# Three edits to the order of work in a one-core diffusion step: output weight splits one query tile later, one tile evicted ahead of the next, a silu table loaded ahead of its use

## The reference

```python
for i in range(DEPTH):
    hp = rms_norm(xp, norm_pre[i, 0]) * (1.0 + sc1_p) + sh1_p
    hs = rms_norm(xs, norm_pre[i, 0]) * (1.0 + sc1_s) + sh1_s
    # i == 0: retention_mixer, i == 1: mla_context / mla_latent (attention), ending in "@ w_out"
    xp = xp + rms_norm(yp, norm_post[i, 0]) * g1_p
    xs = xs + rms_norm(ys, norm_post[i, 0]) * g1_s
    hp = rms_norm(xp, norm_pre[i, 1]) * (1.0 + sc2_p) + sh2_p
    hs = rms_norm(xs, norm_pre[i, 1]) * (1.0 + sc2_s) + sh2_s
    fp = expert_choice_ffn(hp, moe_w_router[i], moe_w_gate[i], moe_w_up[i], moe_w_down[i])
    fs = expert_choice_ffn(hs, moe_w_router[i], moe_w_gate[i], moe_w_up[i], moe_w_down[i])
    xp = xp + rms_norm(fp, norm_post[i, 1]) * g2_p
    xs = xs + rms_norm(fs, norm_post[i, 1]) * g2_s
# an expert: (silu(tokens @ w_gate) * (tokens @ w_up)) @ w_down
```

## Time and profile before

| | us |
|---|---|
| median of three runs | 2384.13 (2383.55 to 2388.96) |
| the profiled execution | 2390.39 |
| its span, first to last instruction | 2388.6 |

### The profile page before, as it was taken

How to read it: one execution, slowest core, us unless ns; L and a number is a source line. 1 busy time by engine, 2 the same in 40 slices (tenths; PEclk the granted TensorE clock), 3 DMA queues, 4 the chain that set the end, 5 groups by cost and what they waited for, 6 DMA issues and landing times.

```text
span 2388.6 us, 27244 instructions
## 1 busy us (share of the span) xinstructions
PE 2265.5 (95%) x10016; PEld 1552.2 (65%) x10016; DVE 1757.0 (74%) x1949; ACT 1273.6 (53%) x1348; POOL 194.9 (8%) x226
## 2 busy tenths in 40 slices
PE   6999999999988999999999798999989999999995
PEld 2866868768654666666666455777656666666663
DVE  2675675766766899999989634455478989999996
ACT  3321312212235777877777434444357777877773
POOL 1000000000022000111000110000120101110001
PEclk9999999999998999999999899999999999999998
DMA  7442434425435999999999400001169999999991
GB/s 270 124 141 92 155 123 133 151 87 176 132 130 197 341 356 362 352 359 345 350 336 362 147 36 3 6 31 37 75 232 352 350 346 361 368 343 345 339 353 60
DMA packets 167652, 529.15 MB, mean 222 GB/s; under 512 B 13525, under 2 KB 22282, under 8 KB 167306
## 3 DMA queue, kind: packets, MB, share of 16 engines
q1 hardware_dynamic: 162954, 515.35, 60.1%
q0 software_dynamic: 2304, 8.39, 1.0%
q10 hardware_dynamic: 2304, 4.20, 0.5%
HBM read 516.72 MB, written 11.17 MB: 221 GB/s over the span
## 4 chain that ended last, share of the span: by engine, by line
PE 89%; DVE 4%; ACT 3%; issue 1%; POOL 1%; DMA 0%; SPq 0%; POOLq 0%; ACTq 0%; DVEq 0%
PE ps L1738 85%; PE ps L1741 4%; POOL SMALL L608 0%; POOL SMALL L607 0%; ACT W_HI L338 0%; DVE IDX L1433 0%; DVE B L1259 0%; DVE X L1260 0%; ACT W L338 0%; DMA REGION<-in_ada_b_dram 0%; DVE MIXREG L1432 0%; DVE B L1234 0%; DVE ROUTE L1435 0%; ACT QN_HI L338 0%; ACT B L751 0%
## 5 line engine op out<-in xcount | busy, mean ns | idle before, releaser
L1470 DVE TENSOR_TENSOR W_LO<-RAW_W,W_HI 128x2048 fp32r<-128x2048 f32 x384 | 867.5, 2288 | 76.4 <-ACT W_HI L338 72.7
L338 ACT ACTIVATE W_HI<-RAW_W 128x2048 fp32r<-128x2048 f32 x384 | 726.9, 1918 | 192.5 <-PE ps L1738 191.5
L1738 PE MATMUL ps<-W_HI,XET_HI 128*80 128x512 f32 x1024 | 322.3, 396 | 7.4 <-DVE B L1504 5.8
L1738 PE MATMUL ps<-W_HI,XET_LO 128*80 128x512 f32 x1024 | 319.6, 393 | 0.0
L1738 PE MATMUL ps<-W_LO,XET_HI 128*80 128x512 f32 x1024 | 319.6, 393 | 0.0
L1738 PEld LDWEIGHTS ps<-W_HI,XET_HI 128*80 128x80 f32 x1024 | 150.9, 148 | 89.1 <-DVE B L1504 6.7
L1738 PEld LDWEIGHTS ps<-W_LO,XET_HI 128*80 128x80 f32 x1024 | 151.9, 148 | 85.8 <-issue 0.9
L1738 PEld LDWEIGHTS ps<-W_HI,XET_LO 128*80 128x80 f32 x1024 | 152.0, 148 | 84.6 <-issue 0.9
L1203 DVE SCALAR_TENSOR_TENSOR ADA_SUM<-ADA_RAW,NCOL,ADA_SUM 128x512 f32<-128x512 f32 x280 | 191.2, 747 | 0.3 <-DMA ADA_RAW<-in_ada_w_dram 0.3
L1738 PE MATMUL ps<-W_HI,HTE_HI 128*80 128x512 f32 x512 | 166.9, 407 | 8.6 <-issue 8.6
L1738 PE MATMUL ps<-W_LO,HTE_HI 128*80 128x512 f32 x512 | 161.2, 396 | 0.0
(11 more groups left out here) (270 smaller groups left out, 3494.3 us busy)
## 6 DMA issues: line engine op xcount, KB each, us to landing
RAW_W<-in_moe_w_gate_dram SPq DMA_DIRECT2D x128, 1024.0 KB, 5.7
RAW_W<-in_moe_w_up_dram SPq DMA_DIRECT2D x128, 1024.0 KB, 6.0
RAW_W<-in_moe_w_down_dram SPq DMA_DIRECT2D x128, 1024.0 KB, 5.2
ADA_RAW<-in_ada_w_dram SPq DMA_DIRECT2D x80, 512.0 KB, 3.6
RING_RAW<-in_ret_w_in_dram SPq DMA_DIRECT2D x48, 512.0 KB, 4.6
W<-in_ada_w_dram SPq DMA_DIRECT2D x4, 2048.0 KB, 13.9
RING_RAW<-in_ret_w_out_dram SPq DMA_DIRECT2D x16, 512.0 KB, 4.8
xn_rows<-B SPq DMA_DIRECT2D x8, 512.0 KB, 12.7
```

The lines of the kernel that those rows point to most:

```text
L338: return nc.scalar.activation(out, in_, ACT.Copy, scale=scale)
L1470: V_.tensor_tensor(W_LO[:, slot], RAW_W[:, slot], W_HI[:, (place + i) % HSLOTS].bitcast(F32), ALU.subtract).then_inc(MS_["lo"], 1)
L1738: return T.matmul(out, lhsT, rhs, start=first, stop=last)
```

## The change

VectorE's `split_out(h, t)` at the end of turn (h, t) becomes `split_out(h, t - 1)`, for t of 1 and more; the four splits after the last head stay, and ScalarE's WO_HI stay in their turns. In the joint, for tile 0 alone, ScalarE's four evictions go ahead of the squares of tile 1, and VectorE's four evictions go between the scaling and the addition of tile 1. In each mixture ScalarE takes the silu of one column of `SSU` (a column that nothing reads any more and that is written anew later) behind the token splits of the first pair, which moves the load of the silu's table to that place.

```diff
@@ -957,6 +957,8 @@
                 split_tokens(0, 0, None)
                 split_tokens(0, 1, None)
+                act.wait_ge(ru_ss, NT * 2 * layer + NT)
+                nc.scalar.activation(SSU[:, 0:1], SSU[:, 0:1], ACT.Silu)
@@ -1009,8 +1011,11 @@
                 for t in range(NT):
                     squares(t + 2)
                     if not layer:
+                        if not t:
+                            norm_act_tile(n + 1, 1, 0, t)
                         norm_squares(n + 1, t + 1, x_ready, NT * n + t + 2)
-                        norm_act_tile(n + 1, 1, 0, t)
+                        if t:
+                            norm_act_tile(n + 1, 1, 0, t)
                         if t >= 2:
                             latent_rows(t - 2)
@@ -1250,13 +1255,15 @@
-            def update(n, t, Y):
+            def update(n, t, Y, between=None):
 
                 if 0 <= t < NT:
                     dve.wait_ge(ru_rstd, NT * n + t + 1)
                     if t == 0:
                         dve.wait_ge(gate_ev, 4 * (n + 1))
                     chain.link(V_.scalar_tensor_tensor(Y[:, t, :], Y[:, t, :], RSTDU[:, t:t + 1], GATE[:, t // NLAT, :], ALU.mult, ALU.mult))
+                    if between:
+                        between()
                     V_.tensor_tensor(X[:, t, :], X[:, t, :], Y[:, t, :], ALU.add).then_inc(x_ready, 1)
@@ -1573,9 +1580,12 @@
                     if not layer:
                         normalise(n + 1, t)
-                    update(n, t + 1, YB2)
-                    if not layer:
-                        norm_dve_tile(n + 1, 1, 0, t)
+                    if not layer and not t:
+                        update(n, t + 1, YB2, lambda: norm_dve_tile(n + 1, 1, 0, 0))
+                    else:
+                        update(n, t + 1, YB2)
+                        if not layer:
+                            norm_dve_tile(n + 1, 1, 0, t)
@@ -1700,7 +1710,8 @@
                         if t == 0 and h:
                             head_out(h - 1, 0)
-                        split_out(h, t)
+                        if t:
+                            split_out(h, t - 1)
                         if h == MH - 1 and t == 0:
                             heads_lo(1, 0, 0, 4)
                 split_out(MH, 0)
```

## The result

The changed kernel takes 2375.84 us, the median of 7 runs (2374.48 to 2380.68). The kernel before, timed beside it, takes 2388.51, also 7 runs (2383.55 to 2389.95). The ratio is 0.9949, with a 95% interval of 0.9940 to 0.9959. The forecast was 2373.2, with a range of 2367.5 to 2378.5. As a ratio to its own starting point it was 2373.2 / 2384.13 = 0.9954. The profiled run of after took 2374.86 us, where that of before took 2390.39; the two are 15.5 us apart.

The account below looks back on a forecast made before the run. TensorE, carrying 89% of the chain that ended last, was taken as the bound. Head 5's 4.96 + head 7's 3.2 + joint's 2.5 + table's 0.2 = 10.9 us off the median 2384.13 gave 2373.2, range 2367.5 to 2378.5.

Parts of the forecast that it names:

- Head 5: Attention head 5: later weight splits remove VectorE's stall, so it lasts as head 6; 4.96 us, 1.63 of it clock.
- Head 7: Attention head 7: TensorE's waits before the transposes of tiles 2 to 4 go; 3.2 us, bounds 2.2 to 3.5.
- the new wait: Head 7: TensorE's products wait for WO_LO of tile 2's block, 0.4 us.
- Joint: First mixture to attention: tile 0's evictions go first, so its products start 2.5 us earlier; 2.5 us taken.
- Table: First expert of each mixture: earlier silu table load gains 0.1 us each, 0.2 in all.
- the move from the profiled execution to the median: Whole kernel: the 10.9 us from the profiled execution, 2390.39, taken equally off the median, 2384.13, giving 2373.2.
- The clock keeps its share: Rival: head 5's 1.63 us absent from the median's executions, joint keeps 1.2; 8.0 us, 2376.1; chance 0.15.
- the order on VectorE does nothing: Rival, heads 5 and 7: WO_HI is late anyway, only joint and table remain; 2.7 us, 2381.4; chance 0.05.
- WO_LO becomes the last thing in head 7: Rival: a new wait in head 7 eats its 3.2 us; gain 7.7, 2376.4; chance 0.08.
- slower case: Joint's products stay at 1.2 GHz past tile 0, through four further tiles; 2401.6 us; chance 0.03.
- the two cases that the sum weighed: Joint: clock returns as long after the restart as before, 2.5 us, or at the same moment, 1.2 us.
- early-clock rival: Joint: the clock returns early in tile 0's products; 13.9 us in all, 2370.2; chance 0.10.

Follow-up runs that it names:

- e1: Kernel before with only VectorE's weight splits one query tile later: 2381.47 us against 2389.45, ratio 0.9964.
- e9: Kernel before with products that nothing reads in three TensorE idles of the attention's preparation: 2386.05 us, ratio 0.9987.
- e8: Changed kernel with VectorE's multiplication ahead of the W_LO that the silu overlaps, first turn of each mixture: 2379.5 us, one run.
- e10: Kernel before with the joint's edit and unread products in the preparation's three idles: 2385.42 us, ratio 0.9986.
- e11: Changed kernel with the multiplication ahead of W_LO and unread products in the idles of preparation, mixtures, last combines and joint: 2366.29 us, ratio 0.9905.

## Why the prediction was right, point by point

- **Head 5**, 4.96 predicted, 4.97 between the two profiled runs. Comparing with the next head was the whole working. It gave the price in that one run: 3.2 us of wait, which every run has, and 1.63 us of clock, which five of nine do not have.
- **Head 7**, 3.2 predicted, 3.43 measured; the new wait was put at 0.4 and is 0.47. The walk by the ends of earlier steps was right to 0.3 us. Both terms together, 8.2, came out as 8.40 between the two profiled runs (heads 5 to 7 in the table) and as 8.0 in e1's time; against the other runs that keep the stall empty it is 6.7 to 9.1.
- **Joint**, 2.5 predicted. The start of the products, worked out from the ends of the evictions, was right (2.39 in after, 2.48 in the idle). Its worth was not one number: tile 1's transposes come 3.02 us earlier in after, the time within either group falls by about 2.3, and on top of e9 by 0.6. In the profiled runs with the whole edit the stretch to the gates is shorter than 70.3 by 2.9 (three runs), 2.2 (e8, 68.13) and 1.1 (e10). The price ahead, 1.35 us later for tile 1, stayed covered: its transposes have no idle.
- **Table**, 0.2 predicted, 2 x 0.13 in the trace.
- **The step that was wrong** was the move from the profiled execution to the median. The prediction found 6.26 us between them and no row that said where, and took off the same 10.9. The table shows two places, by the runs of the lower group that keep the stall (table alone, joint alone). The preparation takes 67.48 us in before and 64.99 there. The twelve products of head 5 take 5.14 in before and 3.51 there; head 7 takes 0.8 more instead, so heads 5 to 7 are worth 7.6 us there, not 8.4. If the runs of after are parted by eye at their gap (four to 2375.84, three from 2378.29), the change is worth about 2384.5 - 2375.0 = 9.5 us in the lower and 2389.8 - 2379.5 = 10.3 in the upper group. So 12.7 us between medians are some 10 of the change and the rest a different share of the groups. That the time came so close was in part luck: two of the three runs at the start were of the lower group, which has 12 of 81. From the third, 2388.96, the same 10.9 would have given 2378.1, just inside the range.
- **The rivals.** *The clock keeps its share* was put down because a stall of 3.2 us is there in every execution. The stall is, the slow products behind it are not, so for head 5 this rival holds in five of nine profiled runs. For the joint, which it put at 1.2, it does not hold in after and in the two runs of the joint alone (2.9 us less to the gates); e10 has 1.1. Its 2376.1 lies nearer to the measured 2375.84 than the forecast does, so the time alone does not decide between them. With head 5's half alone the sum would be 2384.13 - (10.9 - 1.63) = 2374.9, and the four lower runs of after lie at 2374.5 to 2375.8. That the order on VectorE does nothing, and that WO_LO becomes the last thing in head 7, are refuted by e1. The slower case is refuted too: the clock came back inside tile 0's products. It came back earlier than either of the two cases that the sum weighed. In after it is 0.50 until 0.2 us into this stretch, so until 1373.2, 4.8 us behind the restart; before it was 6.1 us (1378.26 less 1372.15).

```profile
1371.00:1373.00 2.00, 2.00 (x4) 0.50 0.00 0
1373.00:1375.00 2.00, 2.00 (x5) 0.95 0.00 0
```

  These two stretches of after, with columns as above, are the 0.63 us by which the joint gave more than the earlier start; something of the early-clock rival was in it. The Trainium skill (TensorE: Matmul & The Clock Gate, What's actually happening) says that the monitor runs freely, does not start anew with a kernel, and that the point at which the clock rises varies for that reason. The preparation agrees that it varies: the same instructions took 65.0 us in one run of the joint alone and 68.9 in another.
- **Open.** Why the joint's edit puts 14 of 17 runs into the lower group is not settled. Of the two profiles of that kernel one is of a lower run, with the short preparation, and one of an upper, with the long one. Nor is it settled why the joint is worth only 0.6 us with the preparation filled; the one profile shows where (the clock in tile 0's transposes), not why. Nor does any run show why head 5's products are slow behind the same idle in some runs and not in others; the filled stall was profiled once.

## What to carry to other kernels

When a queue stands at a wait, look at what is behind it, and find a twin of the stretch without the wait: the difference of the two is the price in that run, clock included. The wait's part of it returns in every run, the clock's part need not. Moving an instruction ahead on one engine helps only if the instruction that it waits for, or that feeds its partner, moves too; half of the joint's edit, by itself, was a loss. Where the runs of a kernel lie in groups, find the stretch that makes them before taking a profiled run's gain off a median.

## What the runs showed of the hardware

- Untouched code differed by 4 us between two runs of the joint alone, in the preparation: 2.3 us of it behind an idle of 1.96 us on TensorE, where the clock was 0.50 for about 10 us instead of under 4, and 1.7 in the twelve products behind an idle of 1.89 us (5.20 against 3.51).
- The same idle of 3.21 us on TensorE in head 5 was followed by the twelve products in 3.51 us in five profiled runs and in 4.97 to 5.19 in four.
- With products that nothing reads in idles of 1.65 to 4.34 us, the granted clock was 1.00 in e11 from 1350 to 1386 and from 1420 to 1490, and the time 9.5 us below the changed kernel; some 0.8 of that can be the multiplication's new place. In e9 and e10, where only the preparation was filled, head 5's products were slow in the profiled run (5.04 and 4.97 us).
- The table load of 1.28 us at its new place is followed at once by the activation, 759.48 to 760.78.
